# Three RWKV steps per item on ScalarE, and the first item's low-rank products and norm later in TensorE's order

## The reference

```python
xs = cols + mu[0] * (prev - cols) + mu[1] * (next - cols)         # token shift; r, k, v are slices of xs
w_log = -softplus(-(w0 + tanh(wd) @ w2)) - 0.5                    # low-rank decay
a  = sigmoid(a0 + ad @ a2)                                        # low-rank rate, per direction
kk = heads(k * rw_kk);  kk = kk * rsqrt(sum(kk * kk) + 1e-12)     # normed key
kd = k[:, :, None, :] * (1.0 + (a - 1.0) * rw_ka)                 # direction's key
bonus = einsum('blhn,bldhn,dhn->blh', rh, kdh, rw_rk)[..., None] * vh
```

## Time and profile before

| what | value |
|---|---|
| median of 3 runs | 3469.64 us (3467.23 to 3474.12) |
| the profiled execution | 3468.2 us, its span 3466.3 us |
| TensorE busy over the span | 3119.8 us (90%) |
| VectorE, ScalarE, GpSimd busy | 2273.6 (66%), 1609.6 (46%), 878.8 us (25%) |
| mean granted TensorE clock | 0.953 |

### The profile page before, as it was taken

The page is one execution under the profiler, slowest core; times in us unless marked ns, Lnnn a source line. Parts: engine busy times, 40 slices in busy tenths (PEclk is TensorE's granted clock), DMA queues, the critical chain, the costliest instruction groups (busy, mean ns, idle before and its releaser), DMA issues. The chain is left out here.

```text
span 3466.3 us, 90868 instructions
## 1 busy us (share of the span) xinstructions
PE 3119.8 (90%) x37105; PEld 2853.6 (82%) x37105; DVE 2273.6 (66%) x4485; ACT 1609.6 (46%) x2917; POOL 878.8 (25%) x1232
## 2 busy tenths in 40 slices
PE   7899989999689999999958971899999999999996
PEld 3887867767579889999947750899999999999996
DVE  4575548996468788888867758555555555555555
ACT  2312756665545444555456530344444444444454
POOL 0110100000056666666622200111211111111213
PEclk8999989999889999999979975899999999999998
DMA  5465335665554554444376622555665655555685
GB/s 178 123 187 175 87 94 190 208 200 160 165 130 113 131 145 106 103 108 109 68 192 187 181 88 85 196 184 184 198 204 189 190 188 190 183 184 187 204 297 186
DMA packets 583428, 561.43 MB, mean 162 GB/s; under 512 B 211550, under 2 KB 527262, under 8 KB 582138
## 3 DMA queue, kind: packets, MB, share of 16 engines
q1 hardware_dynamic: 547084, 447.27, 43.2%
q0 software_dynamic: 36016, 109.52, 10.7%
HBM read 418.33 MB, written 138.33 MB: 161 GB/s over the span
## 5 line engine op out<-in xcount | busy, mean ns | idle before, releaser
L3440 DVE TENSOR_TENSOR exp_wlo<-exp_raw,exp_whi 128x2048 fp32r<-128x2048 f32 x192 | 440.0, 2293 | 362.9 <-ACT exp_whi L3341 355.3
L3341 ACT CAST exp_whi<-exp_raw 128x2048 fp32r<-128x2048 f32 x189 | 359.9, 1904 | 75.7 <-DMA exp_raw<-in_w_up 74.0
L1030 PE MATMUL mix_acc<-proj_hThi,mix_wlo 128*128 128x448 f32 (+3 forms) x920 | 356.3, 387 | 14.5 <-DVE mix_wlo L1398 14.5
L1030 PE MATMUL mix_acc<-proj_hTlo,mix_whi 128*128 128x448 f32 (+3 forms) x920 | 334.7, 364 | 0.0
L1030 PE MATMUL mix_acc<-proj_hThi,mix_whi 128*128 128x448 f32 (+3 forms) x920 | 334.3, 363 | 0.0
L3270 PE MATMUL moe_o<-moe_hidhi,exp_wlo 128*128 128x272 f32 x1024 | 306.8, 300 | 2.6 <-DVE moe_hidlo L3554 2.6
L3270 PE MATMUL moe_g<-moe_xThi,exp_wlo 128*128 128x272 f32 x1024 | 298.9, 292 | 1.0 <-DVE moe_xTlo L3444 1.0
L3270 PE MATMUL moe_o<-moe_hidhi,exp_whi 128*128 128x272 f32 x1024 | 297.1, 290 | 0.0
L3270 PE MATMUL moe_u<-moe_xThi,exp_wlo 128*128 128x272 f32 x1024 | 296.7, 290 | 0.0
L3270 PE MATMUL moe_u<-moe_xThi,exp_whi 128*128 128x272 f32 x1024 | 296.4, 289 | 0.0
L3270 PE MATMUL moe_g<-moe_xThi,exp_whi 128*128 128x272 f32 x1024 | 296.3, 289 | 0.0
(11 more groups left out here) (392 smaller groups left out, 8552.3 us busy)
## 6 DMA issues: line engine op xcount, KB each, us to landing
exp_raw<-in_w_gate SPq DMA_DIRECT2D x64, 1024.0 KB, 5.1
exp_raw<-in_w_up SPq DMA_DIRECT2D x64, 1024.0 KB, 5.1
exp_raw<-in_w_down SPq DMA_DIRECT2D x64, 1024.0 KB, 5.1
scn_plain<-rec SPq DMA_DIRECT2D x68, 384.0 KB, 3.7
rec<-mix_arena SPq DMA_DIRECT2D x24, 896.0 KB, 4.4
proj<-mix_out POOLq DMA_DIRECT2D x88, 224.0 KB, 2.5
scn_grc<-grec SPq DMA_DIRECT2D x136, 128.0 KB, 3.9
mix_arena<-in_w_ada SPq DMA_DIRECT2D x12, 1024.0 KB, 6.8
```

Of the source, the lines that this page charges most:

```text
L1030: mm = pe.matmul(acc[n % ACCS][0:width, 0:tn], wt[:, k, 0:width], hT[hp][:, k, t0:t0 + tn], start=k == 0 and i == 0, stop=k == KD - 1 and ...
L3341: act.copy(w[k % RING][0][:, :, :], raw[k % RAW][:, :, :]).then_inc(hi_done[k % RING], 1)
L3440: dve.tensor_tensor(w[k % RING][1][:, :, :], raw[k % RAW][:, :, :], w[k % RING][0][:, :, :], ALU.subtract).then_inc(lo_done[k % RING], 1)
```

## The change

Three steps per item go from VectorE to ScalarE as activations with a scale (and a bias): the start of the token shift for r (`start_reads`, with its wait until the `bonus_terms` of the item before have read the buffer), the first step of `direction_keys(m, 0)` (`start_direction_keys`, an Identity with scale and bias, ahead of `key_norm_out`) and the start of the bonus (`start_bonus`, behind `totals`). `mix_reads` moves behind `sums` in VectorE's order. `direction_keys(m, 1)` now also waits for `start_bonus`, since it overwrites the key that it reads. In TensorE's order the first item's `low_rank(0, 0)` and `low_rank(0, 1)`, so far at the ends of slots 54 and 55, both stand between the halves of unit 56, and its `key_norm(0)`, so far there, stands between the halves of unit 57, directly ahead of `turn_values(0)`. Loads and stores are the same.

```diff
@@ tensor
                     m = item(n, RW_AT + 1, RW_STEP, RW_N)
-                    if m is not None:
+                    if n == RW_AT + 1:
+                        low_rank(0, 0)
+                        low_rank(0, 1)
+                    elif m is not None:
                         key_norm(m)
                     m = item(n, RW_AT + 2, RW_STEP, RW_N)
+                    if n == RW_AT + 2:
+                        key_norm(0)
                     if m is not None:
                         turn_values(m)
...
                     m = item(n, RW_AT - 1, RW_STEP, RW_N)
-                    if m is not None:
+                    if m:
                         low_rank(m, 0)
                     m = item(n, RW_AT, RW_STEP, RW_N + 1)
                     if m is not None:
-                        if m < RW_N:
+                        if 0 < m < RW_N:
                             low_rank(m, 1)
@@ scalar
+                def start_reads(m):
+                    i, tn = m // NB, MIX_BLOCKS[m % NB][1]
+                    if m:
+                        act.wait_ge(bonus_step, 3 * m)
+                    act.activation(rmix[:, 0:tn], rraw[0][:, 1:tn + 1], ACT.Copy, scale=mus[:, i, 0, 2:3]).then_inc(started, 1)
+
+                def start_direction_keys(m):
+                    i, tn = m // NB, MIX_BLOCKS[m % NB][1]
+                    act.wait_ge(norm_mm, m + 1)
+                    act.wait_ge(a_ready, 2 * m + 1)
+                    act.activation(kd[:, 0:tn], av[0][:, 0:tn], ACT.Identity, scale=par[:, i, 1:2], bias=par[:, i, 8:9]).then_inc(kd_step, 1)
+
+                def start_bonus(m):
+                    i, tn = m // NB, MIX_BLOCKS[m % NB][1]
+                    if m:
+                        act.wait_ge(bonus_mm, m)
+                    act.wait_ge(kd_step, 6 * m + 2)
+                    act.activation(bs[:, 0:tn], kd[:, 0:tn], ACT.Copy, scale=par[:, i, 2:3]).then_inc(bonus_step, 1)
...
                     m = item(n, RW_AT + 2, RW_STEP, RW_N)
                     if m is not None:
+                        start_direction_keys(m)
                         key_norm_out(m)
...
                         low_rank_out(m, 1)
+                        start_reads(m)
...
                         for d in range(2):
                             totals(m, d)
+                        start_bonus(m)
@@ vector
                 def mix_reads(m):
                     i, b = m // NB, m % NB
-                    shift_mix(dve, rmix, rraw[0], mus[:, i, 0, :], b, mixed, rw_base(m) + 2 * mix_ops(b) - 2)
+                    dve.wait_ge(started, 3 * m + 3)
+                    shift_mix(dve, rmix, rraw[0], mus[:, i, 0, :], b, mixed, rw_base(m) + 2 * mix_ops(b) - 2, begun=True)
...
-                    dve.wait_ge(a_ready, u + 1)
-                    if d == 0:
-                        dve.wait_ge(norm_mm, m + 1)
-                    else:
+                    if d:
+                        dve.wait_ge(a_ready, u + 1)
                         dve.wait_ge(rec_dve, u)
-                    dve.tensor_scalar(x, av[d][:, 0:tn], par[:, i, 1:2], par[:, i, 8:9], ALU.mult, ALU.add).then_inc(kd_step, 1)
+                        dve.wait_ge(bonus_step, 3 * m + 1)
+                        dve.tensor_scalar(x, av[d][:, 0:tn], par[:, i, 1:2], par[:, i, 8:9], ALU.mult, ALU.add).then_inc(kd_step, 1)
...
                     if d == 0:
-                        if m:
-                            dve.wait_ge(bonus_mm, m)
-                        dve.tensor_scalar(bs[:, 0:tn], x, par[:, i, 2:3], None, ALU.mult).then_inc(bonus_step, 1)
                         dve.wait_ge(rn_ready, m + 1)
...
                             mix_keys(m)
-                            mix_reads(m)
                     m = item(n, RW_AT + 1, RW_STEP, RW_N)
                     if m is not None:
                         sums(m)
+                        mix_reads(m)
```

More of the change, by code:

```diff
@@ L660, in rw_base @@
         def rw_base(m):
-            return sum(3 * mix_ops(x % NB) - 2 for x in range(m))
+            return sum(3 * mix_ops(x % NB) - 3 for x in range(m))
         def halo(b):
@@ L1542, in mix_values @@
                     i, b = m // NB, m % NB
-                    dve.wait_ge(started, 2 * m + 1)
+                    dve.wait_ge(started, 3 * m + 1)
                     shift_mix(dve, vmix[m % 2], rraw[2], mus[:, i, 2, :], b, mixed, rw_base(m), begun=True)
@@ L1549, in mix_keys @@
                     base = rw_base(m) + mix_ops(b) - 1
-                    dve.wait_ge(started, 2 * m + 2)
+                    dve.wait_ge(started, 3 * m + 2)
                     shift_mix(dve, kmix, rraw[1], mus[:, i, 1, :], b, mixed, base, begun=True)
```

## The result

| | before | after |
|---|---|---|
| median, same chip | 3470.44 us (3467.23 to 3474.12, 4 runs) | 3490.9 us (3488.05 to 3495.54, 4 runs) |
| the profiled execution | 3468.2 us, span 3466.3 | 3488.05 us, span 3486.2 |
| ratio | | 1.0052 [1.0032, 1.0072] |
| clock over the span | 0.953 | 0.950 |

The change makes the kernel slower, by 20.5 us of median in this comparison. The direction was forecast and the size was not: 3490.9 lies 3.9 us above the upper end of the range, and the predicted loss was 9.4. So the change costs 8 to 20 us, some 15 in the middle. 3470 us are 100%, so a tenth of a per cent is 3.5 us.

The account below looks back on a forecast made before the run. TensorE was taken as the bound, VectorE close behind, with ScalarE's chain taking VectorE's place. Item terms summed to +7.7 us, plus 1.7 for the clock: +9.4 on 3468.2, 3477.6, with 1.4 for the median 3479; range 3457 to 3487.

Parts of the forecast that it names:

- ScalarE's chain from K: ScalarE's work after TensorE starts `key_norm`: with Ln's table load behind the Identity, everything later comes 1.95 us later.
- the items with a split: Weight split behind items 3, 8, 13: loss 3.6 us; split inside items 5, 10: loss 2.1 us.
- the string ahead of a new block: Items 4 and 9: SP's loads, then `store_bonus`, then `start_values`, all later with the mix; loss 4.2 us (0 to 6).
- the plain items: Items 1, 2, 6, 7, 11, 12: TensorE's wait before `bonus_sum` nearly vanishes; gain 3.0 us (0 to 5.8).
- the last one: Item 14: its record store is on the path and shifts with the exponentials; loss 1.8 us (0.5 to 2).
- the first item: Item 0: TensorE's saved wait for weights is spent waiting for VectorE and ScalarE; gain 1.0 us (0 to 2.5).
- half of 56 and of 57, 5.0: First item: TensorE's two half units between the low-rank products and the start of `key_norm`, taken as 5.0 us.
- the clock: One more half-clock stretch on TensorE behind the longer waits (none to four); loss 1.7 us.
- Faster, TensorE the only bound: Rival, chance 0.20: VectorE's relief reaches `bonus_sum` everywhere, 14 of 15.9 us of waits go; about 3454 us.
- Ln's load ahead of the Identity: On ScalarE during the wait for `key_norm`: Ln's table load done before the Identity, alone giving about -1 us.
- No change through the SP string: Rival, chance 0.29: the `store_bonus` string costs nothing and the first item gives 2.5; sum +2 to +3, 3471 us.
- Slower through the clock: Rival, chance 0.09: three or four half-clock stretches on TensorE; 3484 to 3487 us.

Follow-up runs that it names:

- filled kernel: The changed kernel with five extra matmuls, overwritten by the next unit, ahead of every `bonus_sum`, the last item's too; 1.0054 against the kernel before.

## Why the prediction was right and wrong

**Right: ScalarE's chain from K takes VectorE's place.** The step that the whole forecast hung on was the load of Ln's table behind the Identity, 1.95 us by the earlier trace rows. It stands there, with Exp at 4.97 where 4.85 was forecast. Putting Ln first took it away in items 0, 3, 10 and 13, and one table for both, which also takes Exp's load off the chain, did so with 14 us of time.

**Right: the items with a split.** +3.6 and +2.1 forecast, +3.6 and +2.2 measured. The reason that this went so well is in the earlier trace rows: from `keep_low` to B nothing else ends later, so a shift of the split is a shift of B.

**Right, with luck on both sides: the string ahead of a new block.** In item 4 SP issued the bonus store at K + 7.6 where it had been at K + 5.4, 2.2 later as forecast (in item 9 1.5 later). What it cost is 2.8 and 2.4 us in items 4 and 9 of `after`, and 0.0 and 0.2 in the third profile of the changed kernel. The mean of 3.5 against 4.2 is thus a mixture of two cases that the forecast did not have. With the early `mix_reads` both items were at 16.3 and 16.4.

**Wrong in size: the plain items and the last one.** -3.0 forecast, -0.3 measured; +1.8 forecast, +0.05 measured. The two misses, 2.7 and 1.8 us, have opposite signs, so that the sum from K to B (+8.7 and +9.1) is right in part by luck. Of the 2.7 us in the plain items 1.8 are what the walk was set against: the six add up to 105.6 us in the one profile it had, and to 103.0 and 102.7 in two more of the unchanged kernel, with 16.4 to 16.8 in three places each. The other 0.9 are the walk, which gave 16.8 (measured 16.5 to 18.0, in the mean 17.2, and 16.77 in item 1 of all three). It had the wait for the `lact` loads at "mostly 0.2"; in `after` it is 1.53 us in item 2 and 1.00 in item 11, the items at 17.96 and 17.84. Against its own profile the forecast was near, -2.5 for -3.0. For item 14 the walk took the record store to be on the path for the full shift; it has 0.45 us in `after`, and nothing in the mean.

**Wrong: the first item**, -1.0 forecast and +0.9 measured. The term "half of 56 and of 57, 5.0" was mis-sized. It counted that stretch at full clock; from the end of the second L1079 (518.05) to K (526.00) it took 7.95 us, with the clock at 0.50 until 522. Landing to 518.05 was 5.8 us where 7.0 were counted, which gives back 1.2 of the 2.95. Over the three profiles of each kernel K comes 0.7 us earlier after the landing (2.1 forecast) and B comes 1.6 later after K (1.1 forecast). The 2.80 us before `turn_values(0)` were forecast as 2.7, and B at K + 19.3 was 19.76. That a shorter wait for the weights buys next to nothing was right.

**Wrong in size: the clock**, +1.7 forecast and +4.2 measured. The prediction counted one more stretch, over a possible none to four. In the mean of three profiles it is 2.5 more than that. In the filled kernel most of the wait at `bonus_sum` is gone and B to K still has 48.4 us, so the stretches hang on those waits in part at most.

**The sum: what failed.** The mechanism was right, and two terms were mis-sized. 14.2 us in the stage against 9.4: 2.5 from the clock (one more half-clock stretch counted, +1.7, measured +4.2), 1.9 from the first item (-1.0 counted for an earlier K, measured +0.9), 0.4 from K to B. The rest of this comparison's 20.5 us, some 6, lies in places that differ as much between two profiles of the unchanged kernel; no experiment assigns it, and its cause stays open. The range was too narrow above for the same reason: its upper end took in four half-clock stretches, and nothing for the first item going the other way or for an execution's own spread.

**The rivals.** *Faster, TensorE the only bound* is what happened once the load was out of the chain and the reads were early: 0.9962, and 0.9951 with `bonus_sum` later. The prediction gave Ln's load ahead of the Identity, alone, about -1 us against before. The nearest run is Ln first, with Exp back at K + 2.90, and it was 7.7 us above (1.0022), with items 5, 8 and 9 held by the later loads and stores. The prediction doesn't show what its -1 was added up from. One table, which takes off more, was 4.9 us below (0.9986, with 1.4 to 8.7 inside its interval). *No change through the SP string* came true for its term in one profile of three; its sum, "+2 to +3", is +2.0 without the 1.7 for the clock and +3.7 with it. *Slower through the clock* is nearest to the first comparison.

## What to carry to other kernels

Before an operation is moved to a less busy engine, write down that engine's queue at the place of the move, table loads included: a cheap function put behind a wait and ahead of one that needs another table pulls the load out of the wait's shadow and onto the chain. Here that, and the later reads with the loads that hang on them, made a loss of about 15 us; asking for the shared table ahead of the wait took 14 us off, and putting the reads back as well showed the gain (13 us below the kernel before) that the move had in it. And the sum of the waits at one instruction is no measure of a change when another instruction stands directly ahead of it: count the waits of both, or the distance between two fixed points.

## What the runs showed of the hardware

- The same kernel takes 3470 us on one chip and 3494 to 3496 on four others (0.7%). Of its profiles, the two on other chips are 23.5 and 29.9 us longer, and 20.6 and 23.1 of that lie behind this stage. Against itself it gave 0.9989 and 1.0009 in two comparisons, and the changed kernel 1.0023, 1.0052 and 1.0055 in three, so such ratios tell a tenth of a per cent at best and can miss by three.
- Half-clock stretches come and go in the same kernel: B to K of the unchanged one summed to 46.2, 49.3 and 49.3 us. Where one falls there, it adds some 1.6 us (3.26 to 4.86 behind item 2 of the third profile), and 2.6 behind item 5 of `after`.
- An Identity with a scale and a bias per partition took 0.75 us on 448 columns (L1263), where a scaled copy takes 0.67. A table load is 1.28 us wherever it stands.
